# Experts' gate and up projections as Strassen's seven products in two column groups, with the last unit's down product between the fifth and the sixth

## The reference

```python
xe = gather(h, idx)                       # 16 experts, each with its own 128 of the 1024 tokens
hid = silu(xe @ w_gate[e]) * (xe @ w_up[e])
ye = (hid @ w_down[e]) * gate[e]
out = zeros.at[idx].add(ye)
```

## Time and profile before

| | |
|---|---|
| median of 3 runs | 4019.66 us (4019.06 to 4022.24) |
| profiled execution, span | 4017.8 us |
| the runs' median above that span | 1.9 us |
| units of moe1 / moe2 | 64 / 16 |

### The profile page before, as it was taken

How to read it: one execution, slowest core, us unless ns; L and a number is a source line. 1 busy time by engine, 2 the same in 40 slices (tenths; PEclk the granted TensorE clock), 3 DMA queues, 4 the chain that set the end, 5 groups by cost and what they waited for, 6 DMA issues and landing times. The chain is left out here.

```text
span 4017.8 us, 48174 instructions
## 1 busy us (share of the span) xinstructions
PE 3714.7 (92%) x19742; PEld 2081.2 (52%) x19742; DVE 1530.6 (38%) x2609; ACT 704.6 (18%) x1506; POOL 444.3 (11%) x500
## 2 busy tenths in 40 slices
PE   7999899987989999999999998999977898869996
PEld 3444488874434444444444444644455898534442
DVE  5656379983810000000000000555166678550001
ACT  2000022210111000010000100412125443112112
POOL 0000000003200000000000000200031776000110
PEclk9999999998989999999999999999988999989998
DMA  7563133216599898888888885412102100219996
GB/s 285 217 257 151 66 125 127 116 42 242 204 341 357 314 311 305 309 310 307 308 308 308 308 300 179 163 49 74 38 0 77 46 4 4 96 53 382 337 332 202
DMA packets 286345, 799.44 MB, mean 199 GB/s; under 512 B 14920, under 2 KB 22096, under 8 KB 271312
## 3 DMA queue, kind: packets, MB, share of 16 engines
q1 hardware_dynamic: 268160, 720.05, 49.5%
q0 software_dynamic: 17280, 74.59, 5.8%
q10 hardware_dynamic: 720, 2.17, 0.2%
HBM read 709.60 MB, written 87.16 MB: 198 GB/s over the span
## 5 line engine op out<-in xcount | busy, mean ns | idle before, releaser
L1508 PE MATMUL banks<-moe_ring,moe_xeT 128*128 128x512 f32 x2560 | 1128.9, 594 | 7.0 <-ACT moe_xeT L1549 7.0
L1508 PEld LDWEIGHTS banks<-moe_ring,moe_xeT 128*128 128x128 f32 x2560 | 481.7, 191 | 584.1 <-issue 581.3
L1604 DVE TENSOR_TENSOR moe_hid<-moe_silu,banks 128x512 f32<-128x512 f32 x80 | 55.0, 688 | 1421.6 <-PE banks L1508 1421.6
L1494 PE MATMUL banks<-moe_ring,moe_hidT 128*128 128x512 f32 x1280 | 562.6, 592 | 1.7 <-DVE moe_ye L1590 1.0
L1494 PEld LDWEIGHTS banks<-moe_ring,moe_hidT 128*128 128x128 f32 x1280 | 240.8, 190 | 293.4 <-issue 291.3
L1789 PE MATMUL banks<-hT,w_in_ring 128*128 128x512 f32 (+3 forms) x976 | 364.0, 535 | 1.9 <-ACT hT L1850 1.1
L512 PE MATMUL banks<-hT,w_in_ring 128*128 128x512 f32 x768 | 339.3, 596 | 1.7 <-PEq L212 1.7
L1789 PEld LDWEIGHTS banks<-hT,w_in_ring 128*128 128x128 f32 (+1 forms) x976 | 183.1, 188 | 181.0 <-issue 170.3
L1568 ACT ACTIVATE moe_silu<-banks 128x512 f32<-128x512 f32 x80 | 47.8, 597 | 1226.3 <-PE banks L1508 1226.2
L512 PEld LDWEIGHTS banks<-hT,w_in_ring 128*128 128x128 f32 x768 | 142.8, 190 | 185.7 <-issue 176.2
L733 PE MATMUL banks<-taps_in,dft 128*128 128x256 f32 x768 | 168.2, 379 | 0.0
(11 more groups left out here) (451 smaller groups left out, 4006.7 us busy)
## 6 DMA issues: line engine op xcount, KB each, us to landing
moe_ring<-d_wg SPq DMA_DIRECT2D x80, 2048.0 KB, 9.4
moe_ring<-d_wu SPq DMA_DIRECT2D x80, 2048.0 KB, 8.3
moe_ring<-d_wd SPq DMA_DIRECT2D x80, 2048.0 KB, 8.3
w_in_ring<-d_w_in SPq DMA_DIRECT2D x9, 2048.0 KB, 10.4
x_normed<-d_mod_w SPq DMA_DIRECT2D x8, 2048.0 KB, 12.5
d_taps<-dft SPq DMA_DIRECT2D x8, 2048.0 KB, 7.4
taps_in<-d_taps SPq DMA_DIRECT2D x8, 2048.0 KB, 9.3
w_in_ring<-d_hy_w_in SPq DMA_DIRECT2D x6, 2048.0 KB, 8.6
```

The lines of the kernel that those rows point to most:

```text
L1494: last = nc.tensor.matmul(m.ps[:, Y_BANK + h, :], hidT[:, c, i * P:(i + 1) * P], down(c)[:, i, h * BANK:(h + 1) * BANK], start=(fc == 0 an ...
L1508: last = nc.tensor.matmul(m.ps[:, 2 * kind + c, :], xeT[:, k, :], up(c, kind)[:, k, :], start=(k == 0), stop=(k == KT - 1))
L1604: nc.vector.tensor_tensor(hid[:, j % 2, :], sg[:, j % 2, :], m.ps[:, 2 + j % 2, :], ALU.mult).then_inc(s.hid, 1)
```

## The change

Gate and up are each a product of 128 tokens by 1024 by 512. It is computed by Strassen's method (the form with seven products): tokens in two halves of 64, contraction in two halves (even and odd steps of 128), inner columns in two halves of 256. One product is four contraction steps of 64 tokens by 256 columns. Gate writes PSUM partitions 0 to 63, up partitions 64 to 127, alternating matmul by matmul, so each uses one half of TensorE's columns. VectorE makes sums of the weights (four per unit, 2048 elements per partition each, one in place), sums of the tokens (four per expert) and the combinations of the products. ScalarE copies the products out in three parts; silu comes after the last combination. The weight ring becomes two tiles of raw gate and up weights, one of them the memory of `m.X`, one tile set of three sums, and **one** tile of down weights. In the new loop `n` is the unit and `j` its place in a pair of experts; `p_mm` counts products, seven a unit, `d_mm` counts finished down products.

The load loop on SyncE:

```diff
+            def load_half(j, a, e):
+                cols = slice(j % nf * EW, (j % nf + 1) * EW)
+                for kind, w in enumerate((d_gate, d_up)):
+                    sp.dma_start(raw[j % 2][:, a, kind * HK:(kind + 1) * HK, :], pick(w, e)[:, a:KT:2, cols]
+                                 ).then_inc(raw_in[j % 2][a], 16)
+
+            def load_down(fc, e):
+                sp.dma_start(wd[:], pick(d_down, e)[:, fc * (EW // P):(fc + 1) * (EW // P), :]).then_inc(s.wd, 16)
 
             def load(turn):
...
                 for j in range(FU):
-                    if not first or j >= 2:
-                        sp.wait_ge(s.g_mm, n - 1)
-                    sp.dma_start(up(c, 0), pick(d_gate, at[eu])[:, :, cols]).then_inc(wg_in[c], 16)
-                    if first and j == 0:
+                    e, fresh = at[j // nf], first and j < 2
+                    if not fresh:
+                        sp.wait_ge(s.p_mm, turn * (PRODUCTS * FU) + PRODUCTS * (j - 2) + 5)
+                    load_half(j, 0, e)
+                    if fresh and j == 0:
                         sp.wait_ge(gathered[0], 16)
-                    if not first or j >= 2:
-                        sp.wait_ge(s.u_mm, n - 1)
-                    sp.dma_start(up(c, 1), pick(d_up, at[eu])[:, :, cols]).then_inc(wu_in[c], 16)
-                    if j:
-                        load_down(pick(d_down, at[(j - 1) // nf]), j - 1, n - 1)
-                    elif not first:
-                        load_down(pick(d_down, before), FU - 1, n - 1)
+                    if not fresh:
+                        sp.wait_ge(s.p_mm, turn * (PRODUCTS * FU) + PRODUCTS * (j - 2) + 7)
+                    load_half(j, 1, e)
+                    if not fresh:
+                        if not first or j > 2:
+                            sp.wait_ge(s.d_mm, turn * FU + j - 2)
+                        load_down((j - 2) % nf, at[(j - 2) // nf])
...
-            load_down(d_down[E - 1], FU - 1, E * nf - 1)
+            for n in (N - 2, N - 1):
+                sp.wait_ge(s.d_mm, n)
+                load_down(n % nf, n // nf)
```

TensorE (`back` is the down product as before, but reads the one tile `wd` after `s.wd`; `rows` is split in two halves of four transposes through one bank):

```diff
+            def product(bank, at, tokens, weights):
+                for k in range(HK):
+                    for kind, out in ((0, LOW), (1, HIGH)):
+                        last = nc.tensor.matmul(m.ps[out, bank, at], tokens(k), weights(kind * HK + k),
+                                                start=(k == 0), stop=(k == HK - 1))
+                last.then_inc(s.p_mm, 1)
...
+                for j in range(FU):
...
+                    pe.wait_ge(s.t, sums + 1)
+                    if started or j:
+                        pe.wait_ge(s.copied, copied - 2)
+                    product(P65_BANK, RIGHT, xsum(1), t(0))
+                    if following:
+                        rows(*following, 0)
+                    pe.wait_ge(s.t, sums + 3)
+                    product(P65_BANK, LEFT, xsum(2), t(1))
+                    pe.wait_ge(s.t, sums + 4)
+                    if started or j:
+                        pe.wait_ge(s.c_all, n)
+                    product(P34_BANK, RIGHT, x(1, HIGH), t(2))
+                    if started or j:
+                        turned(n - 1)
+                        pe.wait_ge(s.copied, copied)
+                    product(PAIR_BANK, RIGHT, x(0, LOW), w(0, LEFT))
+                    if following:
+                        rows(*following, 1)
+                    product(P7_BANK, LEFT, xsum(3), w(0, RIGHT))
+                    if started or j:
+                        back((j - 1) % nf, n - 1, turn * EU + (j - 1) // nf)
+                    product(PAIR_BANK, LEFT, x(1, LOW), w(1, LEFT))
+                    product(P34_BANK, LEFT, xsum(4), w(1, RIGHT))
```

ScalarE and VectorE, per unit:

```diff
+                    part(slice(2, 4), P65_BANK, products + 2)
+                    if started or j:
+                        turned(n - 1)
...
+                    part(slice(4, 5), P7_BANK, products + 5)
+                    part(slice(0, 2), PAIR_BANK, products + 6)
+                    act.wait_ge(s.c22, n + 1)
+                    act.wait_ge(s.c_all, n + 1)
+                    nc.scalar.activation(sg[HIGH], pp[LOW, 0:4, :], ACT.Silu).then_inc(s.act, 1)
...
+            def weight_sums(turn, j):
...
+                v.wait_ge(raw_in[c][0], loads)
+                if after_first(n):
+                    v.wait_ge(s.p_mm, done + 1)
+                nc.vector.tensor_tensor(t1, b12, b11, ALU.subtract).then_inc(s.t, 1)
+                v.wait_ge(raw_in[c][1], loads)
...
+                nc.vector.tensor_tensor(b12, b22, b12, ALU.subtract).then_inc(s.t, 1)
...
+                nc.vector.tensor_tensor(t2, b22, t1, ALU.subtract).then_inc(s.t, 1)
...
+                nc.vector.tensor_tensor(t4, b21, t2, ALU.subtract).then_inc(s.t, 1)
+
+            def combine(turn, j):
...
+                v.wait_ge(s.copied, turn * (COPIES * FU) + COPIES * j + 3)
+                nc.vector.tensor_tensor(pp[:, 0:3:2, :], both(1), pp[:, 0:3:2, :], ALU.add).then_inc(s.c11, 1)
...
+                nc.vector.tensor_tensor(pp[:, 1:3, :], both(2), pp[:, 3:5, :], ALU.add).then_inc(s.rv, 1)
...
+                nc.vector.tensor_tensor(pp[:, 3, :], pp[:, 2, :], pp[:, 3, :], ALU.add).then_inc(s.c22, 1)
...
+                v.wait_ge(s.p_mm, turn * (PRODUCTS * FU) + PRODUCTS * j + 7)
+                nc.vector.tensor_tensor(pp[:, 1:3, :], pp[:, 1:3, :], m.ps[:, P34_BANK, :].rearrange("p (a n) -> p a n", a=2),
+                                        ALU.add).then_inc(s.c_all, 1)
...
+                    if not (final and j == FU - 1):
+                        weight_sums(turn + (j + 1) // FU, (j + 1) % FU)
...
+                        token_sums(*following)
+                    combine(turn, j)
+                    activate(n)
```

More of the change, by code:

```diff
@@ L1382, in experts_stage @@
     ):
[L1383 to L1387, removed]
+        raw = [x.rearrange("p (a k n) -> p a k n", a=2, n=EW) for x in (raw0[:], m.X[:].rearrange("p t d -> p (t d)"))]
+        T_BANK, Y_BANK, ROWS_BANK = 4, 5, 7
+        PAIR_BANK, P65_BANK, P7_BANK, P34_BANK = 0, 1, 2, 3
         gate_v, gate_pe, gate_act = gate_row(nc, m, s, gate, gr, Y_BANK, by)
@@ L1391, in experts_stage, with after_first @@
             ctx_sp, ctx_v, ctx_act = context_ahead(nc, m, s)
+        def after_first(n):
+            return not isinstance(n, int) or n > 0
         @block.sync
         def _(sp):
[L1395 to L1399, removed]
+            pick = lambda w, e: w[e] if isinstance(e, int) else w[ds(e, 1)].rearrange("a p k n -> (a p) k n")
+            def load_half(j, a, e):
[5 more added lines that the diff above has]
+                sp.dma_start(wd[:], pick(d_down, e)[:, fc * (EW // P):(fc + 1) * (EW // P), :]).then_inc(s.wd, 16)
@@ L1463, in turns, with next_expert @@
             body(TURNS - 1, True)
+        def next_expert(turn, j, final):
+            eu = j // nf
+            return None if j % nf < nf - 1 or (final and eu == EU - 1) else (turn + eu, 1 - eu)
         @block.tensor
         def _(pe):
[L1467 to L1476, removed]
@@ L1478, in turned, with rows @@
-            def turned(j, n):
-                pe.wait_ge(s.hid, n + 1)
-                pe.wait_ge(s.ht, n)
+            def rows(turn, eu, h):
+                e = turn * EU + eu
+                if h == 0:
+                    pe.wait_ge(gathered[eu], turn * 16 + 16)
+                if h or after_first(e):
+                    pe.wait_ge(s.xt, e * 2 + h)
+                for j in range(4):
+                    last = nc.tensor.transpose(m.ps[:, ROWS_BANK, j * P:(j + 1) * P],
+                                               xe[:, eu, (4 * h + j) * P:(4 * h + j + 1) * P], m.ident[:])
+                last.then_inc(s.xt_mm, 1)
@@ L1500, in body @@
                 started = not isinstance(turn, int) or turn > 0
[L1501 to L1527, removed]
-                                rows(turn + 1, 0)
-                        if j:
-                            back(j - 1, n - 1, turn * EU + (j - 1) // nf, turn * (FU // 2 * 16) + ((j - 1) // 2 + 1) * 16)
-                        elif started:
-                            back(FU - 1, n - 1, turn * EU - 1, turn * (FU // 2 * 16))
@@ L1533, in body @@
                 if final:
-                    turned(FU - 1, E * nf - 1)
-                    back(FU - 1, E * nf - 1, E - 1, TURNS * (FU // 2 * 16))
+                    turned(N - 1)
+                    back(nf - 1, N - 1, E - 1)
             gate_pe(pe, diag)
-            rows(0, 0, True)
+            for h in range(2):
+                rows(0, 0, h)
             pe.wait_ge(s.gate, 1)
@@ L1577, in body @@
                 if final:
-                    turned(FU - 1, E * nf - 1, True)
+                    turned(N - 1)
             gate_act(act)
-            rows(0, 0)
+            for h in range(2):
+                rows(0, 0, h)
             turns(act, body)
@@ L1585, in _, with token_sums @@
         def _(v):
+            def token_sums(turn, eu):
+                e = turn * EU + eu
```

(9 more changed lines are left out.)

161 lines of the change are left out of this document (98 added, 63 removed).

## The result

| | before | after |
|---|---|---|
| median | 4019.36 us, 4 runs | 4600.65 us, 4 runs (4591.85 to 4608.58) |
| ratio to before | | 1.1444, interval 1.1427 to 1.1461 |
| span of the profiled execution | 4017.8 us | 4590.1 us |
| moe1, first product to last down product | 1355.5 us | 1820.1 us |
| moe2, the same | 349.4 us | 424.8 us |

The change makes the kernel 581 us slower. The forecast was slower, at 4423 (4240 to 4560): the sign and the place are right, the size is not, and the measured time lies outside the range.

What follows compares the result with a forecast made beforehand. PE was taken as the bound, DMA close behind. moe1 +281, moe2 +88, start +26, last down products +3 and early loads +5 make +403 on 4017.8: 4421, as median 4423 us; range 4240 to 4560.

Steps and rivals of the forecast that it cites:

- What decides: Ahead of each unit's down product: PE waits some 3.9 us for the down load, queued behind the seventh product and second half.
- PE's work: On PE per unit: column groups run side by side, a product takes 1.75 us, the whole 19.75 us, 1.3 less than before.
- D: The down product of a unit on PE: 16 matmuls of 0.43 us, 6.9 us.
- T: The transposes of a unit on PE, due after three products of the next unit: 4 x 0.15 = 0.6 us.
- VectorE and ScalarE at nothing: In each unit DVE's 13.1 us and ACT's some 3.1 us are covered by PE's over 19.75 us and cost nothing.
- The cycle of moe2: One unit of moe2: 13.2 + 3.0 + 6.9 + 1.4 + 3.5 = 28.0 us, making its stretch 437.5 us, +88.
- The 3.0 us for the indirect transfers: In moe2's wait for the down load: gather and scatter share the DMA engines, adding 3.0 us a unit, ends 0 and 3.5.
- The cycle of moe1: One moe1 unit: down-load wait 13.2, indirect transfers 0.7, down product 6.9, clock 1.4, sixth and seventh products 3.5: 25.7 us.
- The rival of a slower queue: On the DMA queue: at 342 GB/s the 4.19 MB take 12.3 us, 1.6 more a unit, total 4548; chance 0.12.
- the clock with the down product, 6.9 + 1.4: After each wait: down product 6.9 us, plus 1.4 us because idle time lowers PE's clock, ends 0 and 3.4.
- Start: At each stage's start: second half and sums delay the first product by 12.9 us, to 1141.0 in moe1; twice, +26.
- The rival that the change gains: At the wait ahead of the down product: down weights arrive in time, units take 20.0 and 20.8 us, total 3956; chance 0.06.

## Why the prediction was right in its place and wrong in its size

*What decides.* "Its next load stands on SyncE's queue behind the wait for the unit's *seventh* product and behind the second half of the raw weights" was right; the run with that one order changed takes 542 of 581 us away.

*PE's work.* P = 1.75 was measured as 1.73 to 1.78 us, and the row of 128x64 loads (1702.24 to 1703.89) shows them within the products, so the column groups do run side by side. Changes of the grouping leave no idle time in the rows (transposes recorded until 1710.12, the next product from 1710.04), and the prediction read 0 from such rows. The starts say otherwise. The kernel before, in which the grouping never changes, then the kernel with TensorE's loop written out, where no wait covers it (order of time on TensorE):

```profile
1872.97 0.60 PE L1482 MATMUL banks<-ident,moe_hid 128*128 128x128 f32 x4
1873.41 7.03 PE L1508 MATMUL banks<-moe_ring,moe_xeT 128*128 128x512 f32 x16
...
1881.15 7.03 PE L1494 MATMUL banks<-moe_ring,moe_hidT 128*128 128x512 f32 x16
1888.02 5.31 PE L1508 MATMUL banks<-moe_ring,moe_xeT 128*128 128x512 f32 x12
```
```profile
1890.87 0.66 PE L1507 MATMUL banks<-ident,moe_hid 128*128 128x128 f32 x4
1891.45 1.95 PE L1498 MATMUL banks<-moe_raw,moe_xeT 128*64 128x256 f32 x16
1893.23 1.90 PE L1498 MATMUL banks<-moe_raw,moe_xsums 128*64 128x256 f32 x16
1895.06 7.13 PE L1517 MATMUL banks<-moe_down,moe_hidT 128*128 128x512 f32 x16
1902.12 1.95 PE L1498 MATMUL banks<-moe_raw,moe_xeT 128*64 128x256 f32 x16
```

From start to start the transposes take 0.44 us before and 0.58 after, the down product 6.87 and 7.06; a product takes 1.73 between its like, 1.78 behind a change and 1.83 ahead of one. That is 0.14 + 0.19 + 2 x 0.05 + 2 x 0.10 = 0.63 us in a unit with four changes, some 0.16 each. By the Trainium skill's TensorEngine Tiling (Array Packing), section Tiling Modes, a drain was due there; these rows agree, with a short one. The prediction counted the two changes around D and not the two around T. In the changed kernel those ahead of D are covered by the wait; where no wait is left they take 0.63 us of a unit of 20.04.

*VectorE and ScalarE at nothing*: right. In moe1 the transposes of the hidden values waited 6.8 us in all for DVE, 4.2 of them in the chain at the stage's end, and PE's first product of a stage waits for DVE's sums; elsewhere DVE was never the last to arrive.

*The cycle of moe2*: the forecast stretch was 437.5 us, measured 424.8, which is (424.8 - 17.45)/15 = 27.2 us a cycle in the prediction's own sum (17.45 are its first unit and last chain) against 28.0. The down product with its slow part is 138.9/16 = 8.7 of it, against 8.3, so the rest is 1.2 us shorter than forecast. The 3.0 us for the indirect transfers is the term most likely too large; no run takes it apart.

*The cycle of moe1* is the step that failed: "13.2 + 0.7 + 6.9 + 1.4 + 3.5 = 25.7 us". In the same form of the sum, (1820.1 - 17.45)/63, it was 28.6 us. 63 times 2.9 is 1820.1 - 1636.6 = 183 us, which with moe2's 13 us the other way makes the miss of 169 in the span (572 against 403). The down product of moe1 is 576.4/64 = 9.0 us of the cycle, against 6.9 + 1.4 = 8.3; the rest, from P6 to the next down product, is 28.6 - 9.0 = 19.6 against 3.5 + 13.9 = 17.4. Two terms were mis-sized.
The first is the 13.2 us until the down load lands, built on "a queue that never runs dry moves 393 GB/s" and "Two in a row land at 2.45 + 10.7 = 13.15". The row of 393 came from loads of whole matrices. The halves take even or odd contraction steps, and in moe1 these are slower to read: contiguous halves took 1.9 us off every cycle of moe1 and 126 us off the time. I had both kinds of access in the diff and priced neither. The rival of a slower queue had the right term, with 1.6 us a unit, but another reason, a rate of 342 GB/s read from moe2, and a chance of only 0.12. Of the 2.2 us the other 0.3 are about what the stall at the loop's end comes to, 20/63.
The second is the clock with the down product, 6.9 + 1.4. The runs show 1.6 to 1.7 lost to the idle time, and a down product of 7.1 to 7.2 us at full clock, 0.2 of it from the changes of grouping. The two were sized within 0.3 us each, and the mechanism is shown.

*The range* ended at 4560, just above the 4548 of the rival with the slow queue. That rival comes nearest to what happened, and its own terms had ends too. With the sizes measured afterwards, rows 1.9 for 1.6, the clock 1.6 for 1.4, the down product 7.1 for 6.9, it is 0.7 x 63 = 44 us more, about 4592. A range that is to take in a case has to take in that case's bounds, not its middle.

*Start*: the first product of moe1 came at 1141.96, forecast 1141.0.

*Not foreseen*: the stall at the loop's end, some 20 us of the result; it is in the 28.6.

The rival that the change gains was wrong as to the change and right as to the method: with the queue's order, the loop, the rows, the start and the early loads mended, seven products beat eight by 0.75% (0.6 to 0.9).

## What to carry to other kernels

When an edit cuts the buffers of a ring, write down for each load what it *needs* and what it *stands behind* on its issuing queue; here one issue behind one wait turned a gain of 1.0 us per unit (21.06 to 20.04) into a loss of over 7. A wait on TensorE can cost more than its length: behind 3.48 us of idle the down product started at half clock and took 8.83 us, behind 1.32 us it took 7.13. And when a split of a matrix is free to choose, compare the landing of both splits: in the matrices 2048 wide, contiguous steps of the contraction cost nothing more than the whole, every second one cost 1.9 us a unit.

## What the runs showed that I had not expected

- Reading every second contraction step of a matrix 2048 wide is slower than reading four in a row, with rows of 2 KB in either: 7.7 to 7.8 against 6.8 to 7.0 us to landing. In moe2, with matrices 512 wide, it is not: 8.4 and 9.4 us against 8.4 and 9.7. No run shows why.
- The end of a pass of TensorE's loop cost 4.3 to 4.7 us of standing still, and a product at half clock, in a body of eight units and 56 products; in the kernel before, with 52 matmul instructions a unit in its body in place of 132, no such row is to be seen.
- Forty-eight more matmul instructions per unit, ahead of a wait, made the changed kernel 68 us faster (4600.65 to 4532.45).
- A change between the grouping of 128 columns and that of 64 cost TensorE some 0.16 us, though no idle time is recorded at it. A change of operands within a grouping cost nothing (6.87 us for 16 matmuls of 0.43, with transposes ahead). No run takes the changes out, so this rests on the rows alone.
- GpSimd's scatter takes 3.39 us on its engine in the changed kernel; its group of 32 has a mean of 3156 ns, against 1587 before. No run here looked for the cause.
